# One stream of weights through twelve slots of SBUF instead of four, eight of them lent by idle tiles

## The reference, cut to what matters

```
mx = jnp.split(c_act @ ada_w[i] + ada_b[i], 6, axis=-1)    # c_act: [1, 1024], ada_w[i]: [1024, 6144]
mc = jnp.split(cc_act @ ada_w[i] + ada_b[i], 6, axis=-1)
h_x = modulate(rms_norm(x, norm1_g[i]), mx[0], mx[1])      # mx[2..5]: gates and the second norm
...
out_c, out_x = windowed_gqa_sink(h_x, h_c, ...)            # 16 heads, scores against context and window
x = x + mx[2] * out_x
```

## Time and profile before

| | |
|---|---|
| three runs | 2636.25, 2638.80, 2638.82 us; median 2638.8 |
| profiled execution | 2634.45 us |
| its span in the trace | 2632.6 us |
| granted clock of PE, mean | 0.98 |
| PE, PEld busy | 2511.2 (95%), 2133.2 (81%) |
| DVE, ACT, POOL busy | 1526.1 (58%), 1266.5 (48%), 133.8 (5%) |
| moved by DMA | 398.25 MB, mean 151 GB/s |

### The profile page before, as it was taken

How to read it: one execution, slowest core, us unless ns; L and a number is a source line. 1 busy time by engine, 2 the same in 40 slices (tenths; PEclk the granted TensorE clock), 3 DMA queues, 4 the chain that set the end, 5 groups by cost and what they waited for, 6 DMA issues and landing times.

```text
span 2632.6 us, 42437 instructions
## 1 busy us (share of the span) xinstructions
PE 2511.2 (95%) x15422; PEld 2133.2 (81%) x15422; DVE 1526.1 (58%) x2429; ACT 1266.5 (48%) x1950; POOL 133.8 (5%) x108
## 2 busy tenths in 40 slices
PE   5999999999999998999999999999999999999998
PEld 3735577888878995788888999898888899989887
DVE  2435535333235336666677665768767766576774
ACT  1426633222224343455555458655555545864553
POOL 3000000000000000000000002110000000211000
PEclk8969999999999999999999999999999999999999
DMA  8228742332223341465565555446656455544663
GB/s 262 72 82 269 252 127 74 99 98 92 88 84 120 96 135 49 138 195 180 182 183 162 182 176 159 144 145 191 188 178 190 151 188 171 171 140 146 187 182 121
DMA packets 398654, 398.25 MB, mean 151 GB/s; under 512 B 17361, under 2 KB 396769, under 8 KB 398545
## 3 DMA queue, kind: packets, MB, share of 16 engines
q1 hardware_dynamic: 395680, 390.25, 47.9%
q0 software_dynamic: 2864, 6.57, 0.8%
HBM read 395.72 MB, written 1.05 MB: 151 GB/s over the span
## 4 chain that ended last, share of the span: by engine, by line
PE 79%; DVE 6%; ACT 5%; issue 5%; DMA 3%; POOL 2%; SPq 0%; ACTq 0%; DVEq 0%; POOLq 0%
PE acc L813 27%; PE acc L807 24%; PE acc L809 12%; PE acc L792 4%; DMA raw<-in_ada_w_dram 3%; DVE w_lo L1728 2%; ACT w_hi L1187 2%; PE acc L869 1%; PE wk L936 1%; PE wk L1025 1%; PE wk L963 1%; PE wk L888 1%; PE acc L1156 1%; POOL XC L738 1%; PE wk L878 1%
## 5 line engine op out<-in xcount | busy, mean ns | idle before, releaser
L1728 DVE TENSOR_TENSOR w_lo<-raw,w_hi 128x1024 fp32r<-128x1024 f32 (+1 forms) x656 | 815.7, 1257 | 624.5 <-ACT w_hi L1187 623.2
L1187 ACT CAST w_hi<-raw 128x1024 fp32r<-128x1024 f32 (+1 forms) x656 | 670.2, 1033 | 460.1 <-PE acc L813 229.5
L813 PE MATMUL acc<-h_all,w_hi 128*128 128x256 f32 (+1 forms) x3360 | 747.7, 318 | 20.7 <-DVE w_lo L1728 6.6
L807 PE MATMUL acc<-h_all,w_hi 128*128 128x512 f32 x2016 | 710.4, 397 | 4.5 <-DVE h_all L1837 4.5
L813 PEld LDWEIGHTS acc<-h_all,w_hi 128*128 128x128 f32 x3360 | 561.0, 192 | 65.4 <-issue 14.9
L809 PE MATMUL acc<-h_all,w_lo 128*128 128x256 f32 x2016 | 566.5, 281 | 0.0
L813 PE MATMUL acc<-h_all,w_lo 128*128 128x256 f32 (+1 forms) x1680 | 533.9, 318 | 0.0
L807 PEld LDWEIGHTS acc<-h_all,w_hi 128*128 128x128 f32 x2016 | 379.5, 188 | 93.5 <-issue 4.7
L809 PEld LDWEIGHTS acc<-h_all,w_lo 128*128 128x128 f32 x2016 | 382.6, 190 | 0.2
L813 PEld LDWEIGHTS acc<-h_all,w_lo 128*128 128x128 f32 x1680 | 322.4, 192 | 20.9
L807 PE MATMUL acc<-hid_all,w_hi 128*128 128x512 f32 x880 | 312.4, 398 | 2.9 <-DVE w_lo L1728 2.9
(11 more groups left out here) (342 smaller groups left out, 2498.0 us busy)
## 6 DMA issues: line engine op xcount, KB each, us to landing
raw<-in_w_in_dram SPq DMA_DIRECT2D x100, 512.0 KB, 4.1
raw<-in_ada_w_dram SPq DMA_DIRECT2D x96, 512.0 KB, 5.1
raw<-in_ffn_w_in_dram SPq DMA_DIRECT2D x88, 512.0 KB, 3.6
raw<-in_ffn_w_gate_dram SPq DMA_DIRECT2D x88, 512.0 KB, 3.9
raw<-in_ffn_w_up_dram SPq DMA_DIRECT2D x88, 512.0 KB, 4.0
raw<-in_ffn_w_down_dram SPq DMA_DIRECT2D x80, 512.0 KB, 4.2
raw<-in_ret_w_qkvg_dram SPq DMA_DIRECT2D x48, 512.0 KB, 3.6
raw<-in_ffn_w_out_dram SPq DMA_DIRECT2D x40, 512.0 KB, 3.6
```

The source lines that it names most:

```text
L807: pe.matmul(o, w_hi[:, s, k, c], merged[:, :, kk, t], start=(u == 0 and k == 0), stop=False, skip_group_check=True)
L813: mm = pe.matmul(o, ws[:, s, k, c], xs[:, kk, t], start=(u == 0 and k == 0 and i == 0), stop=(last and k == nk - 1 and i == 2))
L1187: act.copy(w_hi[:, s, 0:nk, :], raw[:, s, 0:nk, :]).then_inc(hi_done, 1)
L1728: dve.tensor_tensor(w_lo[:, s, 0:nk, :], raw[:, s, 0:nk, :], w_hi[:, s, 0:nk, :], ALU.subtract).then_inc(lo_done, 1)
```

## The change

The units of `ada0b` and `ada1` go through a ring of twelve slots. The new tile `ring` is allocated at the place where `raw`, `w_hi` and `w_lo` then lie: its slots 0 to 3 are `raw`, 4 to 7 `w_hi`, 8 to 11 `w_lo`. SP's new function `side_stream` issues the 80 units into slot k % 12, with twelve semaphores `ring_load` of their own. Units 0 to 3 wait for `lo_done` as before, units 4 to 11 for the matmuls of `kv0`'s unit k % 4, later ones for the side unit twelve before. `modulation_unit` reads side units out of `ring`; `load0` takes these 80 units out of the count of `load`, so that the later jobs wait for the right values. The transfers of `wo0` and all that follows keep their conditions.

```diff
--- before.py
+++ after.py
@@ -104,7 +104,7 @@
         self.iters = iters
         self.body = len(unit_chunks)
         self.per = len(ends)
-        self.unit0 = self.block0 = self.unit_step = self.block_step = 0
+        self.unit0 = self.block0 = self.unit_step = self.block_step = self.load0 = 0
         assert self.body % SLOTS == 0 and self.per % 2 == 0
 
     def unit(self, l, it, p):
@@ -126,7 +126,7 @@
 
     def loaded(self, l, it, p):
 
-        return 16 * (self.unit0 // SLOTS + p // SLOTS + 1) + it * (16 * self.body // SLOTS) \
+        return 16 * (self.load0 // SLOTS + p // SLOTS + 1) + it * (16 * self.body // SLOTS) \
             + (l * (16 * self.unit_step // SLOTS) if self.unit_step else 0)
 
 
@@ -178,8 +178,18 @@
     return sum(J.iters * J.body for n, J in JOBS.items() if n in ADA and J.unit0 < JOBS[name].unit0)
 
 
+RINGED = ("ada0b", "ada1")
+RING = 3 * SLOTS
+
+
+def ringed_before(name):
+
+    return sum(J.iters * J.body for n, J in JOBS.items() if n in RINGED and J.unit0 < JOBS[name].unit0)
+
+
 for name in JOBS:
     JOBS[name].split0 = JOBS[name].unit0 - unsplit_before(name)
+    JOBS[name].load0 = JOBS[name].unit0 - ringed_before(name)
 
 
 def job_before(name):
@@ -307,6 +317,8 @@
             return st.enter_context(nc.semaphore(name))
 
 
+        with ExitStack() as on:
+            ring = sb("ring", [P, RING, KCH, COLS], F32, on)
         raw = sb("raw", [P, SLOTS, KCH, COLS])
         w_hi = sb("w_hi", [P, SLOTS, KCH, COLS], F32R)
         w_lo = sb("w_lo", [P, SLOTS, KCH, COLS], F32R)
@@ -408,6 +420,7 @@
 
 
         load = [sem(f"load{k}") for k in range(SLOTS)]
+        ring_load = [sem(f"ring_load{k}") for k in range(RING)]
         hi_done = sem("hi_done")
         lo_done = sem("lo_done")
         units_used = sem("units_used")
@@ -598,6 +611,19 @@
                     return wide[:, :, b * COLS:(b + 1) * COLS]
                 return src
 
+            def side_stream(src):
+
+                kv, first = J["kv0"], J[SIDE[0]].unit0
+                for k in range(SIDE_UNITS):
+                    name, it, p = side_unit(k)
+                    if k < SLOTS:
+                        sp.wait_ge(lo_done, kv.split(None, kv.iters - 1, k) + SLOTS + 1)
+                    elif k < RING:
+                        sp.wait_ge(units_used, kv.unit(None, kv.iters - 1, k % SLOTS) + SLOTS + 1)
+                    else:
+                        sp.wait_ge(units_used, first + k - RING + SLOTS + 1)
+                    sp.dma_start(ring[:, k % RING], src[name](None, it, p)).then_inc(ring_load[k % RING], 16)
+
             def gate_up(gate, up):
                 def src(l, it, p):
                     b, u = divmod(p, 2)
@@ -615,8 +641,7 @@
             wqkv = a["attn_w_qkv"][0]
             stream("q0", plain(wqkv, DC, 0, D))
             stream("kv0", plain(wqkv, DC, D, 512))
-            stream("ada0b", plain(a["ada_w"][0], DC, 2 * D, 4 * D))
-            stream("ada1", plain(a["ada_w"][1], DC))
+            side_stream({"ada0b": plain(a["ada_w"][0], DC, 2 * D, 4 * D), "ada1": plain(a["ada_w"][1], DC)})
             stream("wo0", plain(a["attn_w_o"][0], DC))
             stream("gu0", gate_up(a["ffn_w_in"][0][:, 0:FF], a["ffn_w_in"][0][:, FF:2 * FF]))
             stream("dn0", plain(a["ffn_w_out"][0], FC))
@@ -864,9 +889,15 @@
                 b, u = divmod(p, 2)
                 if u == 0:
                     slot_free(job, None, it, b)
-                pe.wait_ge(load[p % SLOTS], job.loaded(None, it, p))
+                if name in SIDE:
+                    n = job.unit(None, it, p) - J[SIDE[0]].unit0
+                    landed = ring[:, n % RING]
+                    pe.wait_ge(ring_load[n % RING], 16 * (n // RING + 1))
+                else:
+                    landed = raw[:, p % SLOTS]
+                    pe.wait_ge(load[p % SLOTS], job.loaded(None, it, p))
                 for k in range(KCH):
-                    mm = pe.matmul(acc[32 * k:32 * k + 32, b % 2, 0, 0:S], c_wide[:, u * KCH + k, :], raw[:, p % SLOTS, k, :],
+                    mm = pe.matmul(acc[32 * k:32 * k + 32, b % 2, 0, 0:S], c_wide[:, u * KCH + k, :], landed[:, k, :],
                                    start=(u == 0), stop=(u == 1), tile_position=(0, 32 * k), skip_group_check=True)
                 mm.then_inc(units_used, 1)
 
```

## The result

The changed kernel took 2623.93 us in the median of four runs (2620.48 to 2625.20), the kernel before 2637.53 (2636.25 to 2638.82): ratio 0.9946, interval 0.9929 to 0.9964, about 13.6 us or 0.5% faster. The forecast was 2625.2. The profiled execution took 2625.20 us with a span of 2623.4; it is the slowest of the four, so its span shows only 9.2 us less than that of before. All runs with their neighbours, further down, put the gain at 15.7 us.

A forecast was written before the change was run, and what follows sets the result against it. The prediction took PE to bound the attention stage, with 14.9 us of holes, mostly transfer waits. Terms -11.6 - 1.3 - 2.2 + 1.5 = -13.6 us took the median from 2638.8 to 2625.2 us, range 2619 to 2632.6.

The forecast's parts named there:

- part 2: Supply in the first attention: with twelve slots no transfer comes late, so PE's 12 waits for weights go, -11.6 us.
- Part 1: Issue ahead of the attention: units 4 to 11 are transferred earlier, in empty DMA time, which wins nothing there, 0.
- part 6: Handover to `wo0` after the attention: lending `w_hi` and `w_lo` as slots delays none of its transfers or casts, 0.
- part 3: PE's transfer waits in the attention: each hides 0.07 us more than listed, plus 0.5 on weight loads, -1.3 us.
- part 4: PE's clock in the attention: the drop near 202 us goes, the one near 322 is half counted, -2.2 us.
- part 5: New PE waits for DVE and ACT in the attention, once transfers no longer cover them, +1.5 us (0.7 to 7.6).
- Rival A: In the attention the chain PE, DVE, ACT takes over as limit; gain only 7.5 us, 2631.3 us; chance 0.15.
- Rival B: In the attention the transfers stay the limit, twelve slots adding no bandwidth; 2636 to 2639 us; chance 0.09 with D.
- C: A low-clock stretch falls in the products, `wo0` or later, making the kernel slower, 2646.7 us for 43 us; chance 0.03.
- D: SP hangs on some slot, so PE still has only four units ahead; priced with Rival B, chance 0.09 together.
- the clock at 202 us: Sign in the early attention: PE's clock no longer shows 0.50 at 202 us.
- ACT's wait for PE's side units: Sign in the attention: ACT's wait for L869 falls well below 43 us.

The follow-up runs named there:

- e7_no_turns: The changed kernel without the two-column matmuls that turn modulation values between the attention's transposes, values not the reference's; median 2603.90 us, ratio to before 0.9865.
- e5_after_again: The changed kernel run again without an edit; median 2622.62 us, ratio to the kernel before 0.9938.
- e1_ring4: The changed kernel with a ring of four slots instead of twelve, its new tile, semaphores and waits kept; median 2635.41 us, ratio to before 0.9992.
- e8_four_in_gap: The changed kernel with side units 0 to 3 moved into PE's wait ahead of the head normalisation; median 2623.69 us, ratio to before 0.9937.
- e2_ring8: The changed kernel with a ring of eight slots instead of twelve; median 2622.98 us, ratio to the kernel before 0.9940.
- e6_no_transfers: The changed kernel without the 68 side transfers behind the first twelve, values not the reference's; median 2624.54 us, ratio to before 0.9938.
- e3_depth_only: The changed kernel with twelve slots but units 4 to 11 requested as before, each after the unit four earlier was used; median 2626.10 us, ratio to before 0.9951.

## Why the prediction was right

The total was right, but that it agrees to the tenth, 13.6 us forecast and 13.6 measured, is luck: with more runs the gain is 15.7, and three of the terms were off and made up for one another. What was right is the mechanism: four slots ran dry, twelve don't, and PE takes up the time.

*The waits (part 2), -11.6 us:* right; they are gone and nothing took their place. *Part 1 and part 6, nothing:* right; the earlier trace rows against the windows above, and the first cast at 328.50 us behind the copy of the last tile, as before.

*What the list of gaps understates (part 3), -1.3 us:* too small. I counted the overlap ahead of a wait alone. The one wait in the middle of three units that is left in the timeline above shows it whole: 248.29 to 250.61 us is 2.32 us with a listed gap of 0.68, where three units in a row take 1.43:

```profile
265.14 1.50 PE L900 MATMUL acc<-ring,nomask 128*32 128x256 f32 x24
266.57 0.66 PE L980 MATMUL wk<-ident,probs 128*128 128x128 f32 x4
```

A wait between two units costs 0.21 us more than its gap. Ten of the twelve are such; the other two, ahead of the first unit of a half step (196.31 and 242.15 us), hide the 0.07 us of the prediction. That makes 2.2 us. Besides, five groups of L869 in the trace of before are longer than their kind, by 1.2 us in all (0.5 of it the prediction's own estimate), by waits that show on the weight loads or not at all. About 3.4 us in place of 1.3.

*The clock (part 4), -2.2 us:* wrong. Before, it fell twice in the stage; after, twice again, from 208.75 and from 321.5 us, where 16 matmuls of L994 take 3.44 and 3.40 us:

```profile
205.78 1.40 PE L909 MATMUL wk<-sel,ada_s 128*128 128x2 f32 x12
...
321.97 3.40 PE L994 MATMUL acc<-probs_t,v_tok 128*64 128x256 f32 x16
```

The drop at 202 us, behind the idle PE, is gone, as forecast. But another came, where PE is busy without a gap, right behind 24 two-column matmuls. In the nine profiles of the experiments that keep those matmuls, and in that of after, one to three drops stand in the stage; in e7_no_turns, without them, none. That points to the two-column matmuls, but it isn't proof, and they can't be the whole cause. The same 24 matmuls were passed without a drop in the kernel before (L963 at 213.40 us takes 1.95) and in e5_after_again, and so were the runs of 12 and 16 in the middle of the stage. The first drops of before and of e1_ring4 (from 198.25 us) come ahead of any such matmul, among the waits for transfers. So the expectation of e7_no_turns, which has every drop behind such a run, read that too broadly. The 2.2 us were 0. The Trainium skill ("TensorE: Matmul & The Clock Gate", Part 1) says that activity releases the throttle; I read that as "PE without waits keeps its clock", and the rows at 0.50 with PE busy throughout don't bear this reading out. What makes the clock fall there stays open.

*What comes back (part 5), +1.5 us:* too much; about 0.1. The third scores wait 0.40 us (198.11), but ACT's copy costs 0.68 us instead of 0.98. PE's idle time other than for transfers is the same, 3.84 us against 3.83.

The sum by the rows: -11.6 - 3.4 + 0 + 0.1 = -14.9, against 14.34 measured in the stage. Some 0.6 us are not accounted for.

Rival A, that the next chain takes over, isn't reached at today's load of PE: e7_no_turns took 19.65 us off PE and got 17.3 of them. Its chain shows only in places, as in the last steps of e8_four_in_gap. Rival B fell with e2_ring8 and e6_no_transfers, C with the clock behind the stage, D with the waits. The longest stretch at 0.50 in a product there is 8 us in both profiles (781 to 789 us before, 768 to 776 after); the 8 in the last slice of the clock row comes from the last 15 us (0.52 on average), in which PE has only 6.25 us of work. Of the signs, the clock at 202 us came true, but the drop only moved. That the first window would come near 17.5 us missed by the drop in it. ACT's wait for PE's side units seems to have risen from the 43.1 us of the earlier trace rows to 55.7. That is the edge of the window at 165 us, which leaves out the same wait of 15.37 us before and holds it after:

```profile
164.51 0.37 ACT L1384 COPY ada_s<-acc 128x256 f32<-128x256 f32 x1 [15.37 <-PE acc L869]
```

```profile
165.66 0.37 ACT L1415 COPY ada_s<-acc 128x256 f32<-128x256 f32 x1 [15.37 <-PE acc L900]
```

Within the stage the wait fell from 24.2 to 21.5 us; the direction of that sign was right, "well below" was not.

Behind the stage the profile of after takes 2623.4 - 328.50 = 2294.9 us where that of before took 2632.6 - 341.67 = 2290.9. In other profiles of kernels identical there it lies between 2291.4 (e5_after_again) and 2300.2 (e3_depth_only). So its 4.0 us are within the scatter. With the 1.2 us by which the first scores come later (193.06 against 191.89), they leave 9.2 us in the span of the 14.3 in the stage.

## What to carry to other kernels

A queue of slots must cover the longest landing at the fastest rate of use, not the mean of both: four slots gave 8 us on average, less where the units come close together, against landings of 5.1 in the median and 8.4 at most; eight were as good as twelve. When a stall goes, look in its place for what the same engine does around it: a wait costs more than its listed gap, and work that was a filler (the side units in the last steps) may be what covers another chain and keeps the clock. A gain that is read off waits on transfers holds for that execution; two kernels with the same depth showed 6 and 12 us of them. And a sum of waits, or the length of a stage, depends on where it is cut: give it the same first and last event in both kernels.

## What the runs showed of the hardware

The granted clock fell to 0.50 with PE busy for the whole of the window (2.00 of 2.00 us):

```profile
210.00:212.00 2.00, 2.00 (x11) 0.50 1.10 350
322.00:324.00 2.00, 2.00 (x11) 0.50 0.00 1
```

In both windows PE runs matmuls of L994, sixteen of which take 3.4 us there and 1.95 at the full clock. It also stood at 0.50 from 163 to 192 us, with PE busy 29.00 of 29.00 us. A PE that shows as busy didn't by itself keep the clock up here.

Transfers of 0.5 MB landed in 3.4 us at the fastest in e1_ring4 (four slots, median 4.8), and in 7.6 us in the median (10.2 at most) in e3_depth_only, where up to twelve were under way. In the changed kernel, at 5.4 us in the median, supply rose all the same, to 320 GB/s over the first window at a share of 1.00, where it had been 277. In these runs the deeper queues went with longer landings; what they gained was that each request went out sooner.
